# A block kernel's opening sequence, rebuilt: loads from two issuing engines, x in front

## The reference, cut to what matters

```
h = rmsnorm(x, attn_norm[layer])          # x * rsqrt(mean(x*x) + eps) * gain
proj = h @ w_in[layer]                    # 1024 x 6144 weights, split in ten parts
g_f = log_forget(h_ff...)                 # sigmoid of two of the parts, with learned lower bounds
```

## Time and the profile before

| | |
|---|---|
| time of the profiled execution | 2419.63 us |
| its span in the trace | 2417.6 us |
| median of three runs | 2419.88 us |
| TensorE matmul busy | 2348.8 us (97%) |
| VectorE, ScalarE, GpSimd busy | 1263.5, 831.4, 864.9 us |

### The profile page before, as it was taken

The page is one execution under the profiler, slowest core; times in us unless marked ns, Lnnn a source line. Parts: engine busy times, 40 slices in busy tenths (PEclk is TensorE's granted clock), DMA queues, the critical chain, the costliest instruction groups (busy, mean ns, idle before and its releaser), DMA issues.

```text
span 2417.6 us, 28063 instructions
## 1 busy us (share of the span) xinstructions
PE 2348.8 (97%) x11069; PEld 1901.7 (79%) x11069; DVE 1263.5 (52%) x1568; ACT 831.4 (34%) x953; POOL 864.9 (36%) x202
## 2 busy tenths in 40 slices
PE   6999999999999899999999999999999998999998
PEld 5888766788888788887767888888888767888887
DVE  5676345564436555763446644468655653640533
ACT  4332335232222242333343322221325534422332
POOL 3332123343434343321324444444432324343433
PEclk9999999999999999999999999999999999999999
DMA  5332132444445543331223444445773324344442
GB/s 133 86 73 63 35 70 58 92 95 103 88 104 113 145 100 87 70 68 38 58 64 87 96 96 99 92 109 146 155 153 70 70 52 105 70 92 100 87 113 70
DMA packets 192728, 218.04 MB, mean 90 GB/s; under 512 B 14576, under 2 KB 165240, under 8 KB 191864
## 3 DMA queue, kind: packets, MB, share of 16 engines
q1 hardware_dynamic: 192632, 216.68, 40.9%
HBM read 206.92 MB, written 9.73 MB: 90 GB/s over the span
## 4 chain that ended last, share of the span: by engine, by line
issue 70%; POOL 15%; PE 13%; POOLq 0%; DVE 0%; DVEq 0%
POOL w_lo L2672 15%; PE psG L358 4%; PE psG L360 4%; PE psG L359 4%; DVE x2t L2643 0%; POOLq L2669 0%; PE psH L2151 0%; POOLq L2671 0%; DVE y2t L2653 0%; DVEq L2640 0%; PE psH L2138 0%; DVEq L2656 0%; DVEq L105 0%; DVE r4c L2639 0%; POOL ident L869 0%
## 5 line engine op out<-in xcount | busy, mean ns | idle before, releaser
L2672 POOL TENSOR_TENSOR w_lo<-raw,w_hi 128x2048 fp32r<-128x2048 f32 x186 | 858.1, 4614 | 1533.4 <-ACT w_hi L351 1529.1
L358 PE MATMUL psG<-h_hi,w_hi 128*128 128x512 f32 x1640 | 650.0, 396 | 10.6 <-DVE h_lo L489 9.3
L351 ACT CAST w_hi<-raw 128x2048 fp32r<-128x2048 f32 x185 | 353.0, 1908 | 858.8 <-PE psG L360 831.9
L359 PE MATMUL psG<-h_lo,w_hi 128*128 128x512 f32 x1640 | 641.2, 391 | 0.0
L360 PE MATMUL psG<-h_hi,w_lo 128*128 128x512 f32 x1640 | 640.7, 391 | 0.0
L358 PEld LDWEIGHTS psG<-h_hi,w_hi 128*128 128x128 f32 x1640 | 309.1, 188 | 108.6 <-issue 41.5
L360 PEld LDWEIGHTS psG<-h_hi,w_lo 128*128 128x128 f32 x1640 | 309.4, 189 | 65.7
L359 PEld LDWEIGHTS psG<-h_lo,w_hi 128*128 128x128 f32 x1640 | 309.5, 189 | 63.9 <-issue 1.4
L2611 DVE TENSOR_TENSOR hq<-r 128x512 f32<-128x512 f32 x32 | 85.0, 2694 | 150.2 <-ACT r L2377 150.2
L358 PE MATMUL psG<-hid_hi,w_hi 128*128 128x512 f32 x352 | 138.7, 394 | 1.2 <-POOL w_lo L2672 1.2
L359 PE MATMUL psG<-hid_lo,w_hi 128*128 128x512 f32 x352 | 137.4, 390 | 0.0
(11 more groups left out here) (451 smaller groups left out, 3323.4 us busy)
## 6 DMA issues: line engine op xcount, KB each, us to landing
raw<-in_w_in_dram SPq DMA_DIRECT2D x122, 512.0 KB, 6.4
raw<-in_w_gate_dram SPq DMA_DIRECT2D x44, 512.0 KB, 5.9
raw<-in_w_up_dram SPq DMA_DIRECT2D x44, 512.0 KB, 6.0
raw<-in_w_down_dram SPq DMA_DIRECT2D x32, 512.0 KB, 6.4
raw<-in_w_ff_in_dram SPq DMA_DIRECT2D x32, 512.0 KB, 6.2
raw<-in_w_ff_out_dram SPq DMA_DIRECT2D x32, 512.0 KB, 6.0
raw<-in_w_o_dram SPq DMA_DIRECT2D x16, 512.0 KB, 6.0
raw<-in_w_down_dram SPq DMA_DIRECT2D x16, 384.0 KB, 5.3
```

The lines of the kernel that those rows point to most:

```text
L351: act.copy(w_hi[:, s, :], raw[:, s, :]).then_inc(hi_done.sem, 1)
L358: pe.matmul(out, a_hi, b_hi, start=first, stop=False)
L359: pe.matmul(out, a_hi, b_lo, start=False, stop=False)
L2672: pool.tensor_tensor(w_lo[:, s, :], raw[:, s, :], w_hi[:, s, :].bitcast(F32), ALU.subtract)\
```

## The change

- SyncE no longer issues the gains and the first weight unit: it begins with x, then the second weight unit and the two small loads. ScalarE issues the first weight unit and behind it the nine gain loads.
- The low parts of the first two weight units are made on VectorE instead of GpSimd. GpSimd's loop begins with pair 1, behind both.
- h_hi and h_lo are made straight from the transposed tiles in PSUM (for k = 0, and h_lo for k = 1, from xT). Tile 0 is copied to xT by VectorE, tile 1 by ScalarE; tiles 2 to 4 are copied by VectorE after all h_lo and after w_lo of unit 1; tiles 5 to 7 by ScalarE after its h_hi.
- ScalarE casts the second weight unit after h_hi of tile 4.
- ScalarE's squares wait for all copies. The sum over partitions (`sum_pe`) stands in TensorE's order between the two column tiles of unit 1 instead of between unit 0 and unit 1. Unit 1 waits for VectorE's four copies.

```diff
-    def setup_sync(sp):
+    def setup_loads_act(act):
+        w_src(0, 0, first_weights(0), act)
...
         for r, src in rows:
-            sp.dma_start(par_rows[r:r + src.shape[0], :], src).then_inc(ld_par.sem, 16)
-        w_src(0, 0, first_weights(0), sp)
+            act.dma_start(par_rows[r:r + src.shape[0], :], src).then_inc(ld_par.sem, 16)
+
+    def setup_sync(sp):
         for a in range(TB):
             sp.dma_start(x_tok[:, a, :], io["x"].rearrange("a (t p) d -> p (a t) d", p=P)[:, a, :])\
               .then_inc(ld_x[a].sem, 16)
...
         dve.tensor_tensor(small[:, 0:KD], par[:, R_FINAL:R_FINAL + KD], par[:, R_FINAL:R_FINAL + KD], ALU.mult)
+        dve.wait_ge(hi_done.sem, 1)
+        dve.tensor_tensor(w_lo[:, 0, :], raw[:, 0, :], w_hi[:, 0, :].bitcast(F32), ALU.subtract).then_inc(lo_done.sem, 1)
+        dve.wait_ge(x_tr.sem, 1)
+        dve.tensor_copy(xT[:, 0, :], x_bank(0)).then_inc(x_cp.sem, 1)
         for k in range(KD):
-            dve.wait_ge(x_tr.sem, k + 1)
+            gained_lo_of(dve, 0, T_ATTN, k, xT[:, k, :] if k < 2 else x_bank(k), par[:, R_ATTN:R_ATTN + KD])
+        dve.wait_ge(hi_done.sem, 2)
+        dve.tensor_tensor(w_lo[:, 1, :], raw[:, 1, :], w_hi[:, 1, :].bitcast(F32), ALU.subtract).then_inc(lo_done.sem, 1)
+        for k in range(2, KD - 3):
             dve.tensor_copy(xT[:, k, :], x_bank(k)).then_inc(x_cp.sem, 1)
-            if k:
-                gained_lo(dve, 0, T_ATTN, k - 1, xT, par[:, R_ATTN:R_ATTN + KD])
-        gained_lo(dve, 0, T_ATTN, KD - 1, xT, par[:, R_ATTN:R_ATTN + KD])
...
         for u in range(6):
-            if l == 0 and u < 2:
-                pe.wait_ge(x_cp.sem, 2 * u + 2)
-            pe_feature(pe, um + u // 2, u % 2, jm + u // 2, u % 2, h_hi, h_lo, first_tile if u == 0 else None,
-                       by_tile=u == 0)
-            if u == 0:
+            if l == 0 and u == 1:
+                pe.wait_ge(x_cp.sem, KD - 4)
+                pe_feature(pe, um, 1, jm, 1, h_hi, h_lo, tiles=(0,))
+                sum_pe(pe, l, 0, sq)
+                pe_feature(pe, um, 1, jm, 1, h_hi, h_lo, tiles=(1,))
+            else:
+                if l == 0 and u == 0:
+                    pe.wait_ge(n_hi.sem, 2)
+                pe_feature(pe, um + u // 2, u % 2, jm + u // 2, u % 2, h_hi, h_lo, first_tile if u == 0 else None,
+                           by_tile=u == 0)
+            if l > 0 and u == 0:
                 sum_pe(pe, l, 0, sq)
...
         second_pool(pool)
-        with pool.Fori(0, ALL_PAIRS) as m:
+        pool.wait_ge(lo_done.sem, 2 + lo_done.credit)
+        with pool.Fori(1, ALL_PAIRS) as m:
...
     def _(act):
+        setup_loads_act(act)
         split_hi(act, 0, 0)
-        for p in range(4):
-            for k in (2 * p, 2 * p + 1):
-                act.wait_ge(x_cp.sem, k + 1)
-                gained_hi(act, 0, T_ATTN, k, xT, par[:, R_ATTN:R_ATTN + KD])
-            if p == 1:
+        act.wait_ge(setup.sem, 1)
+        act.wait_ge(x_tr.sem, 2)
+        act.copy(xT[:, 1, :], x_bank(1))
+        act.wait_ge(x_cp.sem, 1)
+        for k in range(KD):
+            act.wait_ge(x_tr.sem, k + 1)
+            act.activation(h_hi[:, k, :], x_bank(k) if k else xT[:, 0, :], ACT.Copy,
+                           scale=par[:, R_ATTN + k:R_ATTN + k + 1]).then_inc(n_hi.sem, 1)
+            if k == 4:
                 split_hi(act, 0, 1)
+        for k in range(KD - 3, KD):
+            act.wait_ge(n_lo.sem, n_lo.at(0, T_ATTN + k + 1))
+            act.copy(xT[:, k, :], x_bank(k))
+        act.wait_ge(x_cp.sem, KD - 4)
+        act.drain()
         for p in range(4):
             square_pair(act, 0, 0, p, xT, sq)
```

More of the change, by code:

```diff
@@ L487, in gained_lo, with gained_lo_of @@
     def gained_lo(dve, layer, t0, k, src, gain):
+        gained_lo_of(dve, layer, t0, k, src[:, k, :], gain)
+    def gained_lo_of(dve, layer, t0, k, tile, gain):
         dve.wait_ge(n_hi.sem, n_hi.at(layer, t0 + k + 1))
-        dve.scalar_tensor_tensor(out=h_lo[:, k, :], in0=src[:, k, :], scalar=gain[:, k:k + 1],
+        dve.scalar_tensor_tensor(out=h_lo[:, k, :], in0=tile, scalar=gain[:, k:k + 1],
                                  in1=h_hi[:, k, :].bitcast(F32), op0=ALU.mult, op1=ALU.subtract)\
```

## The result

The changed kernel takes a median of 2423.88 us (2419.31 to 2427.61, 14 runs) and the kernel before 2418.08 us (2413.57 to 2422.13, 14 runs). The ratio is 1.0022, 95% interval 1.0015 to 1.0029: slower by 5.3 us, with 3.6 and 7.0 as ends. That is inside the stated range and on its slow side. It is 0.5 us over the 0.2% (4.84 us) that I called the line between the same and slower, and the interval reaches over that line.

What follows compares the result with a forecast made beforehand. TensorE is 97% busy, so only the opening is at stake; TensorE and the chain from S reach unit 3 together. +0.8 at fixed T and +1.0 for T on 2419.63 give 2421.4, stated as 2421.7 us, range 2414.5 to 2426.

Steps and rivals of the forecast that it cites:

- T: Start of the first transpose of x; forecast 14.0 us, 1.0 later than before, bounds -1.4 and +3.8.
- rival D: Opening loads: queues take packets in turn, T late; 2424.5 us, up to 1.3 more with slow transposes; chance 0.13.
- third case: Opening loads: queues alternate by packet, x is through when half the weights are, the rest shares with second weights; T = 16.85.
- Rival E: Opening loads: weights are served ahead of x and loads simply come earlier, T = 8.8; 2416.5 us; chance 0.04.
- Unit 0 without a stall: TensorE's unit 0: no h_lo held by GpSimd, removing the 3.76 us stall and 1.7 us of low clock.
- S: Start of the sum over partitions; forecast T+24.3 against T+25.8 before, 1.5 us earlier at fixed T.
- The hold in `setup_scalars`: Before unit 3: GpSimd's subtraction holds a small VectorE instruction, about 4 us long; unit 3 starts at S+23.45.
- Rival A: Before unit 3: no hold in setup_scalars, unit 3 at S+19.4, clock stays; 2415.9 us; chance 0.24.
- The clock: At unit 3: 5.2 us of idle TensorE lowers the granted clock to half for 3.4 us; charged 1.7 us.
- Rival B: At unit 3: the hold in setup_scalars is there but the clock does not fall; 2420.0 us; chance 0.09.
- Rival C: Before S: the last fold gets behind GpSimd's subtraction, S later by 4.4 us; 2426.1 us; chance 0.07.
- The sum: Opening at fixed T: -0.9 us for unit 3's earlier start and +1.7 for the lower clock give +0.8.

Runs made afterwards that it cites:

- e1: Changed kernel with the loads of before: SyncE issues gains, first weights, x, second weights; 2417.66 us, ratio 0.9996 to the kernel before.
- e8: Changed kernel with the low part of unit 3's weights made on VectorE in setup_scalars instead of on GpSimd; 2416.76 us, ratio 0.9996 to the kernel before.
- e5: Changed kernel with 20 unused matmuls keeping TensorE busy in front of unit 3; 2418.20 us, ratio 1.0002 to the kernel before.
- e10: As e8, but SyncE issues first weights, x, second weights, and ScalarE the gains; 2406.21 us, ratio 0.9959 to the kernel before.
- e9: Changed kernel with the edits of e1 and e8 together; 2411.18 us, ratio 0.9976 to the kernel before.
- e11: Kernel before with only the loads of e10; 2414.92 us, ratio 0.9997 to the kernel before.
- e2: Kernel before with only the change's loads: x from SyncE, first weights then gains from ScalarE; 2420.99 us, ratio 1.0005 to the kernel before.
- e4: Changed kernel with setup_scalars moved on VectorE behind the Tx of unit 1; 2419.37 us, ratio 1.0005 to the kernel before.
- e6: Changed kernel with SyncE issuing x, first, second weights, and all of h made before the first cast; 2422.98 us, ratio 1.0025 to the kernel before.
- e3: Changed kernel with the nine gains in front of the first weights in ScalarE's queue; 2423.61 us, ratio 1.0026 to the kernel before.

## Why the prediction was right, point by point

**T** was to be 14.0 within 11.65 and 16.85; it was 16.89, and with it the time came out near rival D's 2424.5, to which I gave 0.13. The mechanism, gains behind the weights and the weights sharing with x and then with the second weights, is in the profile, and e1 shows that the loads' order makes T late: T fell to 13.28 with the loads undone. This is the term that I mis-sized most: +1.0 stated, +3.9 measured. I averaged three ways of sharing. The profile counts what each queue moved (packets, MB, share of the 16 engines); q1 is SyncE's and q10 ScalarE's, first from 3 to 8 us, then from 9 to 12:

```profile
q1 hardware_dynamic: 225, 0.79, 59.3%
q10 hardware_dynamic: 550, 0.55, 44.0%
```

```profile
q1 hardware_dynamic: 209, 0.75, 80.1%
q10 hardware_dynamic: 212, 0.21, 23.5%
```

From 9 to 12 us the two queues moved as many packets each, as they would in turn; from 3 to 8 us ScalarE's moved more than twice as many. The page of the Trainium skill that I set beside my cases ("DMA: Bandwidth & Descriptors", "Queues, rings and completion order") has the engines take turns by packet, and the trace agrees with it for the second stretch only. So the third case had its parts wrong. When x was through, at 12 us, ScalarE's queue had moved 0.82 MB and not half of the weights, and their cast began at 15.21, where that case has 2.2+8.05+4.7+1.5 = 16.45. The gains came 1.5 us behind it, at 16.71, and that I had put at nothing. That the two errors leave T within 0.04 us of 16.85 is luck.

The same page of the Trainium skill ("Issuing engines are not separate DMA queues") agrees with the trace: two queues moved 275 to 290 GB/s, between the 221 and the 370 of one. The gain of at most 4.8 us did not come. Rival E, the weights served ahead of x, is out: neither was served ahead.

**Unit 0 without a stall**: right. No h_lo above 0.75 us, and the whole from T to S is 23.5 us (24.3 stated), most of the 0.8 from transposes and h_lo a little closer.

**The hold in `setup_scalars`**: right, at the instruction next to the one named, 4.22 us long, and e8 takes it away. I wrote that a held instruction "starts over" when GpSimd is done; this one ended 0.05 us behind GpSimd and takes 0.18 alone, so that is not what the row shows. From S to unit 3 I had 23.45 and it was 22.71; 0.3 of that is that ScalarE's table load for the root no longer stands behind the sum. Idle 4.70 us (5.2 stated). Rival A did not happen. It stood 4.05 us ahead of the forecast at unit 3, with 1.7 of clock on top, 5.75 in all; e8, which brings it about, has V 5.4 ahead of the changed kernel, with 2.3 of it the clock's by e5.

**The clock**: fell as stated, but for longer, 6.8 us of which 4.7 hit work. The term was 1.7 and measured 2.4 (2.3 by e5). Rival B is out.

**The last fold** began at 39.64, 0.28 ahead of GpSimd's 39.92, with 0.4 to 0.6 stated. Rival C did not happen, and the margin is thin.

**The sum** at fixed T was +0.8, from -0.9 and +1.7. Measured against before, unit 3 is -2.4 at fixed T (S+22.71 and S = T+23.50, so T+46.21 against T+48.65), and the clock adds 2.4: 0.0. These two terms were 1.5 us too high and 0.7 too low, and in part cancel, which is luck as well. With T 3.9 later that is +3.9 by the terms, 3.61 by V, and 5.3 (3.6 to 7.0) by the time. I said +1.8. So the mechanisms were right, and the size that went wrong in the result is T's. By my own line of 0.2% the median is on the side of slower, to which I gave 0.19, and not of the same (0.61), by 0.5 us.

**Behind V** the kernels are the same, yet the profiled executions differ there: from V to the end of the span it is 2320.9 us before, 2317.2 in the changed kernel, 2321.6 in e1, 2317.7 in e5 and 2314.2 in e10. The granted clock of all thirteen profiles, read in stretches of 1 us, settles what differs. Behind V some 41.6 us are at half clock before, 35 in the changed kernel and 25 in e10. With half of that time taken off, 2299.5 to 2301.7 us are left in every one of the thirteen. One of the stretches, which the kernel before ran at half clock and the changed one did not:

```profile
211.30:214.70 3.40, 2.89 (x13) 2.92 (x14) 0.36 (x1) 0.00 (x0) 0.00 (x0) 0.50 0.63 125
```

```profile
211.30:214.70 3.40, 1.56 (x7) 0.94 (x6) 3.40 (x8) 1.26 (x2) 0.00 (x0) 1.00 0.76 182
```

Each such stretch is worth about 1.7 us, and how many there are varies between executions of one kernel: of the executions of the kernel before beside e9 to e11, one with a span of 2411.1 us had a mean granted clock of 0.993 and one with 2419.6 us had 0.990. That is most of why single times scatter by 8 us, and why a time and V may differ by 2 or 3 us (e2, e4, e10). Open is whether the place where the opening ends changes their number on average as well: the mean granted clock is 0.994 over e10's five executions and 0.992 over the twenty of before beside them, so a part of e10's 9.9 us may lie there.

## What to carry to other kernels

Moving work forward pays only up to the next place where another chain arrives at the same time; find that place first, and price the change from there (here TensorE's work moved forward by 8 us at fixed T and unit 3 by 2.4). When one engine's work moves, look at which small instructions of another engine now fall beside a long subtraction on GpSimd. Give loads the order in which the first product needs them, all of its inputs, and do not put the smallest of them behind the largest.

## What I had not expected of the hardware

A load of 48 KB in nine DMAs, alone in its queue, was there by 5.2 us with nothing beside it, and at 9.4 to 10.8 us with x and weights running from the other queue (e6, e10). By what rule they are kept waiting is not shown: turns of one packet each would have brought them in sooner than the 15 packets against 459 of e10. The instruction held for 4.22 us in the changed kernel is a TENSOR_SCALAR of 128x32 with a single tensor input, so GpSimd's subtraction holds not only two-input instructions. The timeline of the kernel before shows it already, in a line that I had not used (0.48 us otherwise, GpSimd busy from 65.25 to 69.93):

```profile
65.39 4.83 DVE L1271 TENSOR_SCALAR Kf<-Kf,cur 128x512 f32<-128x512 f32 x1
```

It does not hold every one: the reciprocal of 128x512 began at 40.99 beside a subtraction that ran from 39.03 to 43.62 and took the 3.35 us that it takes in each of its five places. And idle TensorE of 4.7 us brought 6.8 us at half clock where 3.76 us had brought 3.4, with 12 us bringing 10 to 13.5 (e3, e6). The length of the idle time does not settle it: 3.82 us brought 6.8 too (e4).
